# Two-layer hybrid trunk step in fp32: seven block products in place of eight for pairs of feed-forward weight strips

## What is computed

```python
mod = silu(c) @ w_ada[l] + b_ada[l]          # six chunks of 1024: shift1, scale1, gate1, shift2, scale2, gate2
h  = modulated_norm(x, norm_mix, shift1, scale1)
...
x  = x + gate1[:, None, :] * (merged @ w_out)
h2 = modulated_norm(x, norm_ffn, shift2, scale2)
f_gate, f_up = jnp.split(h2 @ w_ffn_in, 2, axis=-1)          # 1024 x 5632
x  = x + gate2[:, None, :] * ((silu(f_gate) * f_up) @ w_ffn_out)   # 2816 x 1024
```

## Time and profile before

| | |
|---|---|
| median of 3 runs | 2985.23 us (2985.14 to 2987.11) |
| profiled execution | 2975.47 us |
| its span (first to last instruction) | 2973.6 us |
| granted TensorE clock, mean | 0.974 |
| busy, share of span: TensorE / weight loads / GpSimd / VectorE / ScalarE | 95% / 86% / 54% / 48% / 25% |
| matmuls | 17704 |
| feed-forward part, layer 0 and layer 1 | about 1145 to 1589 us, and 2515 to 2957 us |

### The profile page before, as it was taken

How to read it: one execution, slowest core, us unless ns; L and a number is a source line. 1 busy time by engine, 2 the same in 40 slices (tenths; PEclk the granted TensorE clock), 3 DMA queues, 4 the chain that set the end, 5 groups by cost and what they waited for, 6 DMA issues and landing times.

```text
span 2973.6 us, 42669 instructions
## 1 busy us (share of the span) xinstructions
PE 2823.4 (95%) x17704; PEld 2550.6 (86%) x17704; DVE 1430.7 (48%) x2267; ACT 754.1 (25%) x1411; POOL 1596.7 (54%) x596
## 2 busy tenths in 40 slices
PE   7889899989999999999999989999999999999998
PEld 2349687978888999999998869797988998999998
DVE  6555685664545235477646571542455425411113
ACT  3442112215564112000112110414555212000110
POOL 0426132364434776788875507075333675777775
PEclk9979999999999999999999999899999999999999
DMA  5422242231111323345422213021111233322222
GB/s 218 138 96 95 92 161 88 96 92 43 52 46 61 114 70 123 113 156 163 144 91 88 92 59 102 5 93 54 46 52 52 84 96 107 98 73 78 72 78 79
DMA packets 80093, 272.12 MB, mean 92 GB/s; under 512 B 8955, under 2 KB 14715, under 8 KB 78108
## 3 DMA queue, kind: packets, MB, share of 16 engines
q1 hardware_dynamic: 48124, 168.77, 17.8%
q10 hardware_dynamic: 31776, 100.62, 9.8%
HBM read 245.76 MB, written 23.59 MB: 91 GB/s over the span
## 4 chain that ended last, share of the span: by engine, by line
PE 80%; DVE 9%; ACT 4%; issue 2%; DVEq 1%; DMA 1%; POOLq 1%; POOL 1%; ACTq 0%; SPq 0%
PE PS L499 46%; PE PS L843 9%; PE PS L562 4%; PE PS L636 3%; PE PS L892 2%; PE PS L509 2%; PE PS L790 2%; DVE adap L1483 2%; PE PS L864 1%; PE PS L774 1%; POOLq L482 1%; PE PS L602 1%; POOL wlo L483 1%; PE PS L759 1%; PE PS L869 1%
## 5 line engine op out<-in xcount | busy, mean ns | idle before, releaser
L481 POOL TENSOR_SCALAR whi<-wraw 128x1024 fp32r<-128x1024 f32 x284 | 819.2, 2884 | 1146.6 <-PE PS L499 635.5
L483 POOL TENSOR_TENSOR wlo<-wraw,whi 128x1024 fp32r<-128x1024 f32 x292 | 734.4, 2515 | 83.3 <-ACT whi L1246 38.9
L499 PE MATMUL PS<-hhi,whi 128*128 128x320 f32 x2432 | 556.7, 310 | 15.7 <-POOL wlo L483 15.7
L499 PE MATMUL PS<-hhi,wlo 128*128 128x320 f32 x2432 | 554.7, 309 | 0.0
L499 PE MATMUL PS<-hlo,whi 128*128 128x320 f32 x2432 | 554.7, 309 | 0.0
L499 PEld LDWEIGHTS PS<-hhi,whi 128*128 128x128 f32 x2432 | 407.2, 188 | 18.4 <-POOL wlo L483 11.5
L499 PEld LDWEIGHTS PS<-hlo,whi 128*128 128x128 f32 x2432 | 407.8, 188 | 0.0
L499 PEld LDWEIGHTS PS<-hhi,wlo 128*128 128x128 f32 x2432 | 407.4, 188 | 0.0
L1483 DVE CUSTOM_DVE_ANT_0 adap<-ada,cond 128x1024 f32<-128x1024 f32 x176 | 333.2, 1893 | 36.1 <-DMA ada<-in_w_ada 14.7
L1401 ACT ACTIVATE silu<-PS 128x640 f32<-128x640 f32 x44 | 31.2, 708 | 659.1 <-PE PS L499 655.8
L1915 DVE TENSOR_TENSOR gact<-silu,PS 128x640 f32<-128x640 f32 x44 | 36.1, 821 | 333.3 <-ACT silu L1401 333.3
(11 more groups left out here) (294 smaller groups left out, 5022.8 us busy)
## 6 DMA issues: line engine op xcount, KB each, us to landing
wraw<-in_w_strips SPq DMA_DIRECT2D x292, 512.0 KB, 3.5
ada<-in_w_ada ACTq DMA_DIRECT2D x80, 512.0 KB, 4.6
spectra<-hst ACTq DMA_DIRECT2D x48, 256.0 KB, 2.1
hld<-spectra ACTq DMA_DIRECT2D x8, 768.0 KB, 5.0
hld<-spectra ACTq DMA_DIRECT2D x12, 512.0 KB, 3.6
part<-hacc ACTq DMA_DIRECT2D x8, 640.0 KB, 3.5
macc<-part ACTq DMA_DIRECT2D x8, 640.0 KB, 4.1
pada<-in_w_ada ACTq DMA_DIRECT2D x8, 512.0 KB, 3.7
```

Of the source, the lines that this page charges most:

```text
L481: nc.gpsimd.tensor_scalar(hi, raw, 1.0, None, ALU.mult)
L483: nc.gpsimd.tensor_tensor(lo, raw, hi, ALU.subtract).then_inc(w_split, 1)
L499: ins = pe.matmul(out[:, h, :], w[:, kt, :], mv[:, h * HALF:(h + 1) * HALF], start=start and m == 0, stop=stop and m == 2)
```

## The change

**Block products.** 20 of the 22 pairs of a layer (all but the first two, `PLAIN = 2`) no longer multiply strip by strip. With the gate strip's two k-halves G1 and G2, the up strip's U1 and U2, and h in four blocks (k-half 1 or 2, token half 1 or 2: B11, B12, B21, B22), seven products are made in place of eight:

p1 = G1 B11, p2 = G2 B21, p5 = (U1 + U2)(B12 - B11), p6 = (U1 + U2 - G1)(B22 - B12 + B11), p3 = (G2 - U1 - U2 + G1) B22, p7 = (G1 - U1)(B22 - B12), p4 = U2 (B21 - B22 + B12 - B11).

The gate sums are p1 + p2 and p1 + p6 + p5 + p3, the up sums p1 + p6 + p7 + p4 and p1 + p6 + p7 + p5. A product is 4 k-tiles x 3 terms = 12 matmuls of 320 columns in one PSUM bank. They run in the order 1, 2, 5, 6, 3, 7 and, after the next pair's 1, 4 (`run_of`).

**Who makes the parts.** VectorE makes the four sums of strip halves (`strip_sums`, L2109, the last in place in `wraw`), the four sums of h blocks once a layer (`h_sums`), and the sums of products out of PSUM (`pair_sums`). ScalarE makes each block's high part (`block_high`, `bhi`, four buffers, L1538). The low parts `blo` of blocks 1 and 2 are VectorE's (`strip_low`, L2115), those of 5, 6, 3, 7 and 4 GpSimd's (L587). SP loads a strip into a buffer once the sums that read the old one are made and its last low part is split.

**Other moves.** The feed-forward part has four runs of pairs, each with its output strips (`PARTS = (6, 6, 5, 5)`), in place of two; the first output strip of each has its high part made by ScalarE, as have eight strips of layer 1's neighbourhood stage. The norm before it also stores h unsplit (`hf`, L1150). The modulation's dots lie otherwise: both layers make scale2 and shift2 in their neighbourhood stage, gate1 in their differential stage and gate2 in their merge; only layer 1's first 16 are made in layer 0's feed-forward part, one after each add into x. Some semaphores are joined.

```diff
-            for n in range(DEPTH * STRIPS):
+            for lay in range(DEPTH):
+                for idx in range(S_FFN + 2 * PLAIN):
+                    strip_split(lay * STRIPS + idx)
+                for f in range(len(PARTS)):
+                    for c, name in run_of(f):
+                        i = PRODUCTS[lay, c, name]
+                        if name in "12":
+                            continue
+                        pool.wait_ge(w_bhi, i + 1)
+                        nc.gpsimd.tensor_tensor(blo[i % 4][:, :, :], block_of(lay, c, name)[0], bhi[i % 4][:, :, :],
+                                                ALU.subtract).then_inc(w_blo, 1)
+                    for idx in range(S_IN[f] + 2 * PARTS[f], S_IN[f + 1]):
+                        strip_split(lay * STRIPS + idx)
...
+                def block_product(f, c, name):
...
+                    pe.wait_ge(*block_ready(lay, c, name))
+                    if REUSED[lay, c, name] is not None:
+                        pe.wait_ge(*bank_free(lay, *REUSED[lay, c, name]))
...
+                    for k in range(KB):
...
+                        for m, (w, mv) in enumerate(((bhi[i % 4], hi), (bhi[i % 4], lo), (blo[i % 4], hi))):
+                            ins = pe.matmul(PS[:, bank, 0:HALF], w[:, k, :], mv,
+                                            start=k == m == 0, stop=k == KB - 1 and m == 2)
...
+                if nrm % 2:
+                    for sgm, cols in SEGMENTS[i // KD]:
+                        ins = A(hf[:, k, cols], tn[k % 3][:, cols], ACT.Identity, bias=mod[:, shift + k, sgm:sgm + 1])
+                    ins.then_inc(s_hf, 1)
...
+                def block_high(c, name):
+
+                    i = PRODUCTS[lay, c, name]
+                    src, came = block_of(lay, c, name)
+                    act.wait_ge(*came)
+                    if i >= 4:
+                        act.wait_ge(s_prod, i - 3)
+                    A(bhi[i % 4][:, :, :], src, ACT.Copy).then_inc(w_bhi, 1)
...
+                def pair_sums(f, c):
...
+                    dve.wait_ge(*product_done(lay, c, "2"))
+                    V.tensor_tensor(g1[:, h0], first1[:, :], p2, ALU.add).then_inc(s_part, 1)
+                    if more:
+                        strip_sums(c + 1, 0)
+                        strip_low(c + 1, "1")
+                    if c > max(PAIR0[f], PLAIN):
+                        product_low(f, c - 1)
+                    if more:
+                        strip_sums(c + 1, 1)
+                    dve.drain()
+                    dve.wait_ge(*product_done(lay, c, "6"))
+                    V.tensor_tensor(mid[:, :], first1[:, :], p6, ALU.add).then_inc(s_part, 1)
...
-                    if lay == 0:
-                        if n == 0:
-                            dve.wait_ge(s_cond[2], 16)
-                        ada_dot(3, n, 2 * KD + n)
...
+                    if n in (1, 3, 5):
+                        if n == 1:
+                            dve.wait_ge(s_cond[2], 16 * (lay + 1))
+                        ada_dot(3, KD * lay + n // 2, 2 * KD + n // 2)
+                for k in range(3, KD):
+                    ada_dot(3, KD * lay + k, 2 * KD + k)
...
-                for f in range(2):
-                    for j in range(KFH):
...
+                for f, nk in enumerate(PARTS):
+                    for c in range(max(PAIR0[f], PLAIN), PAIR0[f + 1]):
+                        pair_sums(f, c)
+                    product_low(f, PAIR0[f + 1] - 1)
```

More of the change, by code:

```diff
@@ L490, in tiles_of @@
                 n = lay * STRIPS + idx
-                wh, wl = whi[n % 2], wlo[n % 3]
-                pe.wait_ge(w_split, n + 1)
+                wh, wl = whi[ORDINAL[n] % 2], wlo[n % 3]
+                pe.wait_ge(w_split, ORDINAL[n] + 1)
                 for t, (kt, hi, lo, p, start, stop, done) in enumerate(work):
-                    if ready is not None and ready(t) is not None:
-                        pe.wait_ge(*ready(t))
+                    for wait in ready(t) if ready is not None else ():
+                        pe.wait_ge(*wait)
                     out = pair(p)
@@ L1372, in _ @@
                 early_out(3)
+                act.dma_start(cond[4][:, :, :], conds).then_inc(s_cond[3], 16)
+                for k in range(ADA_SLOTS[4]):
+                    ada_load(4, KD * lay + k, (lay, N_ADA2 + k))
                 for i in range(4):
@@ L1395, in _ @@
[L1395 to L1410 removed]
+                if lay == 0:
+                    act.dma_start(cond[2][:, :, :], conds).then_inc(s_cond[1], 16)
+                    for k in range(ADA_SLOTS[2]):
+                        ada_load(2, k, LATE[k])
@@ L1867, in _ @@
                                         ALU.subtract).then_inc(s_mg, 1)
+                    if i == 0:
+                        dve.wait_ge(s_cond[3], 16 * (lay + 1))
+                    for k in range(2 * i, 2 * i + 2):
+                        ada_dot(4, KD * lay + k, N_ADA2 + k)
+                modulation(lay, N_ADA2, N_ADA)
                 def add_to_x(m, p, gate, done, hs=(0, 1)):
@@ new lines, in strip_sums @@
+                def strip_sums(c, which):
+                    f = max(i for i in range(len(PARTS)) if PAIR0[i] <= c)
+                    n = lay * STRIPS + S_IN[f] + 2 * (c - PAIR0[f])
+                    first, second = wraw[n % 3], wraw[(n + 1) % 3]
+                    g = (KF - PLAIN) * lay + c - PLAIN
+                    dst, x0, x1, op, name = (
+                        (bsum[0][:, :, :], second[:, 0:4, :], second[:, 4:8, :], ALU.add, "5"),
+                        (bsum[1][:, :, :], bsum[0][:, :, :], first[:, 0:4, :], ALU.subtract, "6"),
+                        (bsum[2][:, :, :], first[:, 4:8, :], bsum[1][:, :, :], ALU.subtract, "3"),
+                        (second[:, 0:4, :], first[:, 0:4, :], second[:, 0:4, :], ALU.subtract, "7"))[which]
+                    if which < 2:
+                        m = n + 1 - which
+                        dve.wait_ge(w_in[m % 3], 16 * (m // 3 + 1))
+                    if g and which < 3:
+                        before = (lay, c - 1) if c > PLAIN else (lay - 1, KF - 1)
+                        dve.wait_ge(*block_ready(before[0], before[1], name))
+                    dve.drain()
+                    V.tensor_tensor(dst, x0, x1, op).then_inc(w_add, 1)
```

582 lines of the change are left out of this document (377 added, 205 removed).

## The result

The change takes **2910.1 us** (median of 4 runs, 2908.3 to 2917.1), the kernel before, run beside it, 2986.2 us (4 runs, 2985.1 to 2988.1): a ratio of 0.975 with an interval of 0.973 to 0.977. The prediction was 2936 us, 2918 to 2990: right in sign, 26 us too high, and the time lies 8 us under the range.

A forecast was written before the change was run, and what follows sets the result against it. The prediction took TensorE, busy for 95% of the span, as the bound. Matmuls -70.4, VectorE's pace +12, norm +11 and dots -2 sum to -49.4 us, so 2985.2 becomes 2936 us, range 2918 to 2990.

The forecast's parts named there:

- Matmuls taken out: Feed-forward pairs of both layers: 480 matmuls fewer at 0.1467 us each, -70.4 us.
- VectorE's pace: Feed-forward runs: VectorE, shut out by GpSimd at the shared port, sets the pace; +12 us, bounds 0 and +69.
- I laid three pairs out in time: Feed-forward runs: a product-by-product timeline from instruction prices, giving VectorE 13.8 us a pair against TensorE's 12.3.
- Norm and start of the feed-forward part: Norm before feed-forward: ScalarE writes h twice, VectorE makes the h sums; +11 us in both layers, bounds 3 and 20.
- Dots: Modulation dots, neighbourhood and differential stages: layer 0 gains, layer 1 pays, merge dots cost nothing; -2 us, bounds -10 and +13.8.
- More and smaller parts: Feed-forward output phases: four in place of two, 16 more adds into x a layer; nothing, bounds 0 and +8.
- The baseline: Whole kernel before: the forecast started from the median of the runs shown, 2985.2 us.
- formula: Ends of feed-forward runs: last activation at 3.5 + 13.6 + 13.8 (N - 2) + 6.3 us, N pairs, against TensorE's need.
- the hidden case with the best dots: Whole kernel: VectorE's lag hidden and dots at their best bound, 2918 us, the low end of the range.
- the gap at each product: Rival, feed-forward: 280 products each cost a 0.1 us gap, 28 us, 2964; chance 0.18 shared with paces of 14.3 to 15.4.
- the port that makes it slower: Rival, feed-forward: GpSimd low parts shut VectorE out fully, 15.9 us a pair, 2993; decides from about 15.6; slower 0.12.
- All is hidden: Rival, feed-forward: GpSimd's short operations fall beside VectorE's PSUM operations, pace stays 12.3 us, 2924 us; chance 0.13.

The follow-up runs named there:

- a_eight: The change with product 4 of each of the 40 pairs made twice into the same bank, 96 matmuls a pair again: 2973.8 us, ratio 0.9975 to the kernel before.
- a_noread: The change with GpSimd's low parts of blocks replaced by a zero fill that writes SBUF and reads none: 2910.45 us, ratio 0.977 to the kernel before.
- a_vec2: The change with the first strip sum of each pair made twice on VectorE: 2948.3 us, ratio 0.988 to the kernel before.
- b_same: The kernel before, unchanged, timed and profiled once more: 2982.95 us, ratio 1.000.
- b_da: The kernel before with only layer 0's differential dots moved: three between the rope steps, five behind them, their loads moving too: 2976.2 us, ratio 0.998.
- b_na: The kernel before with only the loads of layer 0's neighbourhood dots issued two steps later on ScalarE's queue: 2976.2 us, ratio 0.998.
- a_parts: The change with runs of 6, 5, 5, 6 activations in place of 6, 6, 5, 5: 2916.0 us, ratio 0.978 to the kernel before.
- a_same: The change, unchanged, timed and profiled once more: 2909.95 us, ratio 0.977 to the kernel before.
- a_low_pool: The change with all seven low parts of a pair on GpSimd, none on VectorE: 2915.9 us, ratio 0.977 to the kernel before.

## Why the prediction was right or wrong

The time came out lower than forecast by 26 us. By size, what was wrong: the dots (14.5 us too little), the norm (9 too much), VectorE's lag (4 to 6.5 too much) and the median that it started from (4 too much); the smaller parts (5 to 6, put at nothing) went the other way.

**Matmuls taken out (-70.4): right.** 480 fewer, at 0.1467 to 0.1468 us, and where TensorE sets the pace no gap at the products. a_eight puts 480 back and costs 63.7 us; the lag that it hides fits the rest.

**VectorE's pace (+12): the mechanism right, the size not.** GpSimd's low part of 512 and its hold of the port were right to 0.05 us. The step that failed is "I laid three pairs out in time": it gave 13.8 us a pair. VectorE's own 10.1 us stand, and what it is shut out for is 2.0 to 2.3 us (a_noread against the change) to 2.6 (the pace of 12.65 less those), not 3.7. My reading of why, which no run tests: whatever was shut out once starts as GpSimd ends, and GpSimd then waits for ScalarE's next high part (168 us in all before `blo<-bsum`), so the two fall into step. The path lost 12.65 - 12.33 = 0.3 us a pair in three runs and nothing in the second; worked out run by run from the chain it is 2.9 us in layer 0 and 2.6 in layer 1: **+5.5**. The second profile adds 2.5 to that, in layer 0's second run, whose 504 matmuls take 1317.30 - 1240.76 = 76.5 us there and not 74.0:

```profile
1240.76 31.69 PE PS L1086 x216
...
1317.30 37.23 PE PS L606 x252
```

So the lag is 5.5 to 8.0 us. a_vec2 shows that VectorE stood at its limit, and was not well under it: there the prediction's picture was right, its margin not.

**Norm and start of the feed-forward part (+11): about +2.** The failing step is "Doubled, that is 1.5 and 1.06: it becomes the pace" (0.56 doubled is 1.12, which would have made it worse). The timeline of ScalarE in the norm of the change:

```profile
1104.50 0.73 ACT L1150 ACTIVATE hf<-tn,mod 128x128 f32<-128x128 f32 x2
1105.14 0.73 ACT L1146 ACTIVATE hhi<-tn,mod 128x128 fp32r<-128x128 f32 x2
...
1121.29 0.55 ACT L1146 ACTIVATE hhi<-tn,mod 128x320 fp32r<-128x320 f32 x1
1121.75 0.55 ACT L1150 ACTIVATE hf<-tn,mod 128x320 f32<-128x320 f32 x1
```

Back to back, starts are 0.64 and 0.45 us apart, less than the 0.73 and 0.55 that each row lasts: a step is 1.28 and 0.91 us, against the 1.17 and 0.92 before. The second half costs nothing, the first about 1 us. The third strip's wait behind it grew from 2.10 us to 3.21:

```profile
2473.95 0.56 PE L606 MATMUL PS<-hhi,whi 128*128 128x320 f32 x2 [3.21 <-POOL wlo L576]
```

That 1.1 is near the 1.5 foretold, but a wait of 0.4 us that the fourth strip had is gone. From the last output tile to the end of the first two pairs it is 52.9 and 53.0 us, 51.8 before: +1.1 and +1.2. Durations of single instructions, added up, were the wrong price for a row of them.

**Dots (-2): much too little.** The stages around them give, the repeats compared, -9.2 and -8.6 in layer 0, -2.6 and -1.2 in layer 1, and +2.7 and +2.4 in what follows: **-16.5 us** (-11 by the first two profiles, whose starts differ by 3.9 us). a_eight gives the same from the other side: its gain of 7.5, with the 2.3 of the norm, 5 to 6 of the smaller parts and some 1 of lag left in its runs, makes 16 to 17. The step that failed is "So layer 0 gains 4.5 and layer 1 loses 2.7" and, for the neighbourhood stage, half away in layer 0 and half into layer 1: it took layer 0's surplus from one profile (13.8 us; 18.5 in b_same), gave only part of it back, and made layer 1 pay for its new dots. The runs show that the dots, placed so, cost the two stages nothing: it was where they and their loads stood in the queues. b_da alone gains 8.5 to 10.5 us in its stage, b_na alone 7.3 to 9.9. Layer 0's two stages come out at 168.7 and 163.4 us, layer 1's time without any dots. Layer 1 itself became 2.3 to 2.6 us shorter in the neighbourhood stage though dots came in; I put that down to its eight high parts on ScalarE, which relieve GpSimd, but no run separates them. The eight dots of the merge, predicted at nothing, go with a merge that is 1.2 us longer in each layer (134.99 against 133.76 us in layer 0); no run tests whether they are the cause, nor what the rest of the 2.4 to 2.7 is.

**More and smaller parts (0, bounds 0 to +8): inside the bounds.** The last output phase is shorter (five strips for each of eight tiles, not eleven), so less of TensorE's work lies over the norm's first steps. From the first matmul of layer 0's last output phase to layer 1's first turns it is 180.5 us and 1130 matmuls before, 143.3 us and 842 in the change: 37.2 us less where the matmuls alone give 42.2, so +5.0 us (+3.8 by the repeats), and +1.3 at the end of layer 1. a_parts takes 0.9 us off the end of layer 1, as expected, and nothing that repeats off layer 0's; that all of it is this is worked out from marks, not shown.

**The baseline.** The forecast stood on 2985.2; 28 runs of the same kernel have their median at 2981.3. That is 4 us of the 26.

Summed against a_same and b_same (-71.7 us between their spans), with the lag and the smaller parts as the repeats have them: -70.4 + 8.0 + 2.3 + 5.2 - 16.5 + 0.8 (start) = -70.6, so 1 us stays unexplained.

Two of the prediction's sums do not come out as written. By its formula a pace of 15.9 gives waits of 59 to 77 us in both layers, by whether the first pair of a run is slowed too, and not its 6, 11, 9 and 9 (69); and the hidden case with the best dots is 2924 - 8 = 2916, not 2918. Neither changes the forecast, and 2910 lies outside either way.

**Of the rivals**, the gap at each product and the port that makes it slower fell (six pairs at 12.33 us each leave no room for a gap, and a_eight costs less than its matmuls, not more; the pace is 12.65, far from the 15.6 that the second needs). "All is hidden", 2924, came nearest, for the wrong reason: about half of the lag is there, and the dots and the norm made up for it, which is luck.

## What to carry to other kernels

Beside a full TensorE, VectorE was busy for 85 to 87% here, and time added to it showed in full (38 us for 31 added). Time taken from it did not: a_noread and a_low_pool took the lag out of the runs, and most or all of it came back as waits at their ends. A load that takes ScalarE's queue 0.33 us to issue can cost far more by what stands behind it in that queue (7 to 10 us for one stage's loads in b_na); look there first, with the list of who waits for whom, before pricing the instruction. And profile the kernel before twice where a forecast rests on differences of a few us between stages: one of its two profiles was 8 us shorter for no reason in the code.

## What the runs showed of the hardware

A GpSimd subtraction of 512 elements, which reads SBUF, holds a VectorE operation with two SBUF inputs up by as much as 1.15 us of its 1.30; a fill of the same tile, which only writes, by none (0.695 us at most over 120 sums). A GpSimd copy of 1024 elements (2.77 us) holds one up only until about 0.9 us after its start. A lone ScalarE activation of 320 elements lasts 0.56 us, but in an unbroken row the next starts 0.45 us later; for two of 128 and 192 elements it is 0.75 and 0.64 us.
